# The opening of a hybrid Hyena, grouped-query and neighbourhood attention block: the order of its first loads, its filter taps, and the first halves of two projection tiles

## What is computed

```python
mod_l = (silu(c) @ w_mod + b_mod)          # 6 x 1024 values; c_ctx gives mod_c in the same way
sh1, sc1, gt1, sh2, sc2, gt2 = split(mod_l, 6)
pl = modulate(rms_norm(x, g_mix), sh1, sc1) @ w_in      # h @ w_in, 768 + 512 + 2*128 + 3*256 columns
pc = modulate(rms_norm(ctx, g_mix), csh1, csc1) @ w_in
hy_l, q_l, k_l, v_l, nq_l, nk_l, nv_l = split_proj(pl)
...
# the implicit filter of the Hyena part: a small network over the positions
h = sin(om * (z @ w1 + b1)); h = sin(om * (h @ w2 + b2)); h = sin(om * (h @ w3 + b3))
h = h @ w_out_f                                          # 1024 x 512: 256 forward, 256 backward taps
h_fwd, h_bwd = h[:, :256] * decay, h[:, 256:] * decay
filt = concatenate([h_fwd, zeros(1), h_bwd[:0:-1]])
u = short_conv(hy_l, conv_w, conv_b); v, x1, x2 = split(u, 3); v = v * x1
hyo = x2 * (fft_long_conv(v, filt) + v * skip)
# then: attention of two kinds, output projection, residual, SwiGLU, residual, final rms_norm
```

## Time and profile before

| | us |
|---|---|
| median of 3 runs | 1409.38 |
| lowest and highest | 1409.36, 1409.6 |
| the profiled execution | 1410.57 |
| its span in the trace | 1408.8 |

### The profile page before, as it was taken

One profiled execution on the slowest core, in us unless ns is written; L12 is line 12 of the kernel. 1 busy time (PEld: TensorE's weight loads), 2 busy tenths in 40 slices (PEclk: granted clock), 3 DMA queues, 4 the chain that ended last, 5 costly groups with the idle time before them and its releaser, 6 DMA issues. The chain is left out here.

```text
span 1408.8 us, 24040 instructions
## 1 busy us (share of the span) xinstructions
PE 1341.5 (95%) x8353; PEld 737.0 (52%) x8353; DVE 1003.3 (71%) x1612; ACT 686.8 (49%) x1307; POOL 237.4 (17%) x165
## 2 busy tenths in 40 slices
PE   4989999999888899999899999999999999999997
PEld 0274566444566677777654544444444444444442
DVE  2587677779788889989643697666766665676387
ACT  0442223534577788888630555444444445412235
POOL 0000000133331660000000213333333330000001
PEclk9999999999999999999999999999999999999999
DMA  6916510154140120210011303222222223698953
GB/s 208 375 39 247 201 60 31 61 134 150 31 109 0 32 90 30 63 26 0 2 45 45 90 1 102 78 82 75 81 79 78 82 82 104 229 339 290 339 190 137
DMA packets 119612, 156.25 MB, mean 111 GB/s; under 512 B 18707, under 2 KB 80381, under 8 KB 118269
## 3 DMA queue, kind: packets, MB, share of 16 engines
q1 hardware_dynamic: 113419, 152.32, 32.4%
q10 hardware_dynamic: 6130, 3.11, 0.8%
HBM read 132.98 MB, written 22.42 MB: 110 GB/s over the span
## 5 line engine op out<-in xcount | busy, mean ns | idle before, releaser
L986 PE MATMUL PS<-arena 128*128 128x512 f16 (+6 forms) x7048 | 1218.2, 331 | 35.3 <-DMA arena<-in_hy_f_wout 9.9
L986 PEld LDWEIGHTS PS<-arena 128*128 128x128 f16 (+3 forms) x7048 | 607.5, 102 | 588.4 <-issue 48.2
L2332 DVE SCALAR_TENSOR_TENSOR arena<-arena 128x512 f16<-128x512 f32 x148 | 120.8, 823 | 76.4 <-ACT arena L1747 76.4
L1747 ACT ACTIVATE arena<-arena 128x512 f16<-128x512 f32 x140 | 87.6, 629 | 130.4 <-PE PS L986 130.4
L2268 DVE SCALAR_TENSOR_TENSOR arena<-PS,arena 128x512 f16<-128x512 f32 (+2 forms) x256 | 140.0, 598 | 4.4 <-ACT arena L1686 2.3
L1686 ACT ACTIVATE arena<-PS 128x512 f16<-128x512 f32 (+2 forms) x256 | 118.5, 531 | 49.8 <-PE PS L1271 49.8
L1271 PE MATMUL PS<-arena 128*128 128x128 f32 x864 | 115.2, 278 | 7.4 <-ACT arena L1676 6.0
L1676 ACT ACTIVATE arena<-PS,arena 128x1280 f32<-128x1280 f32 (+1 forms) x96 | 118.0, 1230 | 1.1
L1271 PEld LDWEIGHTS PS<-arena 128*128 128x128 f32 x864 | 93.0, 141 | 44.4 <-ACT arena L1676 43.2
L2260 DVE TENSOR_REDUCE arena<-PS 128x1 f32<-128x1280 f32 x64 | 95.5, 1492 | 23.0 <-PE PS L986 23.0
L1859 ACT ACTIVATE arena<-arena 128x512 f16<-128x512 f32 x77 | 48.1, 629 | 127.3 <-DVE arena L2481 73.4
(11 more groups left out here) (179 smaller groups left out, 1070.7 us busy)
## 6 DMA issues: line engine op xcount, KB each, us to landing
arena<-in_w_ffn_out SPq DMA_DIRECT2D x121, 256.0 KB, 4.8
arena<-in_w_mod SPq DMA_DIRECT2D x24, 1024.0 KB, 6.4
arena<-in_w_ffn_in SPq DMA_DIRECT2D x88, 256.0 KB, 3.0
arena<-in_w_in SPq DMA_DIRECT2D x9, 1024.0 KB, 5.2
left_operands<-arena SPq DMA_DIRECT2D x33, 256.0 KB, 2.2
arena<-left_operands SPq DMA_DIRECT2D x3, 2816.0 KB, 15.1
arena<-in_x SPq DMA_DIRECT2D x2, 2048.0 KB, 17.4
arena<-cst_fwd SPq DMA_DIRECT2D x4, 1024.0 KB, 11.7
```

The lines of the kernel that those rows point to most:

```text
L986: return pe.matmul(out, lhsT, rhs, start=start, stop=stop, skip_group_check=True)
L1747: act.activation(aS[n % RING][:, 0], weight_block(p, b), ACT.Copy, scale=WS).then_inc(blk_hi, 1)
L2332: dve.scalar_tensor_tensor(dst[:, 1], src, WS, dst[:, 0], ALU.mult, ALU.subtract).then_inc(blk_lo, 1)
```

## The change

It has six parts, all in the opening.

1. **Loads.** The vectors c and c_ctx and the identity have a semaphore of their own (`c_in`) and are alone ahead of the chunks. Four `w_mod` chunks follow at once, without the wait for the filter loads; then the other six small loads, and x in front of chunks 5 and 6, `rest` in front of chunk 7. ACT issues three filter loads first, then loads its SiLU table on a dummy value, takes SiLU of c, and only then issues the other seven.
2. **PE's order.** It transposes 16 rows for c alone, takes `modulation(0)` and `(1)`, transposes all 106 rows, takes `modulation(2)`, and only then the first filter layer. The others are spread as shown below.
3. **Taps.** Seven of the eight tap products use the sum and the difference of the filter's output weights (`fwo_sums`, two additions on DVE), so that DVE needs one multiplication per tile in place of three instructions; the first tile keeps the old way.
4. **h.** The first four turns stand ahead of and between the tap products, and DVE splits them between its tap multiplications. `layer_argument`, `normalise_x` and `modulation_gain` move with them.
5. **Hyena.** The first 512 tokens of tiles 0 and 1 (24 products each) are taken after the first six `filter_sums`, with turns 12 to 19 between them; the turns use banks 1 and 3 from n = 12 on (`h_bank`). The second six `filter_sums` follow with nothing between them, then the other halves of both tiles.
6. **Small ones.** DVE takes the first late chunk ahead of the second `filter_spectrum`, the first Hyena weights are split after n = 7 (before: 15), and ACT's two negated copies stand at n = 4.

```diff
-            for dst, src in first:
-                sp.dma_start(dst, src).then_inc(first_in, 16)
+            for dst, src in with_c:
+                sp.dma_start(dst, src).then_inc(c_in, 16)
             n_of = dict.fromkeys(CHUNKS, 0)
             for c in range(N_EARLY):
-                if c == 1:
-
-                    sp.wait_ge(small_in, N_SMALL)
-                if c == 6:
+                if c == 4:
+                    for dst, src in first:
+                        sp.dma_start(dst, src).then_inc(first_in, 16)
+                if c in (5, 6):
+                    i = c - 5
+                    sp.dma_start(xs[:, 4 * i:4 * i + 4], x_rows[:, 4 * i:4 * i + 4]).then_inc(x_in[i], 16)
+                if c == 7:
                     for dst, src in rest:
                         sp.dma_start(dst, src).then_inc(rest_in, 16)
...
-            for dst, src in small:
+            for dst, src in small[:3]:
                 act.dma_start(dst, src).then_inc(small_in, 16)
+            act.wait_ge(pool_own, 1)
+            act.activation(warm, neghalf[:, 0:1], ACT.Silu)
...
+            for dst, src in small[3:]:
+                act.dma_start(dst, src).then_inc(small_in, 16)
...
-            for ct in range(4):
+            pe.wait_ge(hT_f, 20)
+            for ct in range(2):
+                hyena(ct, (1,))
+            for ct in range(2, 4):
                 hyena(ct)
...
+            def tap_tile(nt):
+
+                dve.wait_ge(taps_mm, nt + 1)
+                ps = PS[:, 6 + nt % 2].rearrange("p (a k) -> p a k", a=2)
+                dec = decay[:, nt].rearrange("p (a k) -> p a k", a=2)
+                if nt:
+
+                    dve.tensor_tensor(filt[:, :, nt], ps, dec, ALU.mult).then_inc(taps_rdy, 1)
+                    return
...
             for nt in range(NT):
...
+                tap_tile(nt)
+                if nt == 1:
+                    normalise_x(1, 4, 8)
+                if nt == 3:
+                    mean_x(8, 10)
+                if 2 <= nt < 6:
+                    split_first(nt - 2)
+            normalise_x(2, 8, 10)
```

More of the change, by code:

```diff
@@ L580, in build @@
         ]
+        N_C = len(with_c) * 16
         N_FIRST = len(first) * 16
@@ L1137, in hyena @@
                         for o in others:
-                            for half in range(2):
+                            for half in halves:
                                 ins = mm(PS[:, 2 * b + half, :], w[:, part, k, b * P:b * P + P],
@@ L1141, in hyena, with modulation_columns @@
                                          k == 0 and part + o == 0, k == KD - 1 and part == 1)
-                ins.then_inc(hy_mm, 1)
+                    if between is not None and k % 2 == 1:
+                        turn_h(between + k // 2)
+                if 1 in halves:
+                    ins.then_inc(hy_mm, 1)
+            def modulation_columns(g):
+                pe.wait_ge(mrow_rdy, g + 1)
+                for i in range(8):
+                    o = 16 * g + 2 * i
+                    ins = pe.transpose(PS[:, 5, o:o + 2], mrow[0:2, g, i * P:i * P + P], ident[0:2, 0:2])
+                return ins
@@ new lines, in _ @@
+            pe.wait_ge(silu_rdy, 1)
+            modulation(0)
+            modulation(1)
+            pe.wait_ge(first_in, N_FIRST)
+            pe.transpose(PS[:, 5, 0:N_ROWS], rows[0:N_ROWS], ident[0:N_ROWS, 0:N_ROWS]).then_inc(cols_mm, 1)
+            modulation(2)
+            pe.wait_ge(small_in, N_SMALL)
+            filter_layer(0)
+            modulation(3)
+            modulation(4)
+            pe.wait_ge(cols_rdy, 3)
+            modulation_columns(0)
+            filter_layer(1)
+            modulation(5)
@@ new lines, in _ @@
+            modulation(6)
+            filter_layer(2)
+            modulation(7)
+            turn_h(0)
+            turn_h(1)
+            modulation_columns(1).then_inc(mcol_mm, 1)
+            pe.wait_ge(mlp_h, 3)
+            for nt in range(NT):
+                taps(nt)
+                if nt in (2, 4):
+                    turn_h(1 + nt // 2)
+            n = 4
+            for part, count in enumerate((2, 2, 1, 1, 1, 1)):
+                for i in range(count):
+                    turn_h(n)
+                    n = n + 1
+                if part == 0:
+                    arrived(pe, chunk_index("ff", 0))
+                    pe.wait_ge(mod_rdy, 1)
+                    pe.wait_ge(taps_rdy, NT)
+                if part == 4:
+                    pe.wait_ge(even_part, 2)
+                filter_sums(0, part)
```

228 lines of the change are left out of this document (105 added, 123 removed).

## The result

The changed kernel takes 1422.4 us (1422.1 to 1425.8, 4 runs) against 1409.5 before (1409.4 to 1410.3, 4 runs): a ratio of 1.0096, interval 1.0078 to 1.0113. I had forecast 1401.8, with 1393 to 1413 as the range. The prediction was wrong in sign and outside its range.

A forecast was written before the change was run, and what follows sets the result against it. PE was taken as the engine to follow in the opening. Checkpoint 30 + 81.3 + 6 = 117.3 against 126.9, 9.6 earlier; less 2 for the queue, 7.6: profiled 1410.6 to 1403.0, median 1401.8 us, range 1393 to 1413.

The forecast's parts named there:

- PE before the filter loads: Opening: chunk 0 in at 8.4, three modulation chunks and a transpose follow, so PE reaches the filter layer at 21.9.
- slow start: PE's modulation records after a long idle take 0.86 instead of 0.43 for the first 5.7 us, costing 2.8.
- When the filter loads are in: Landing of the seven filter loads issued at about 5.3: taken as 30, with 21.5 as lower bound and 38.3 as late case.
- S: Time in us when all filter loads are in, taken as 30 (18.48 before); the gain at the checkpoint is 39.6 - S.
- checkpoint: End of the second Hyena tile, where ACT starts on it: 126.9 before, forecast 117.3, before the queue's charge.
- SP's queue goes first: Rival: filter loads move only when SP's queue is dry, S = 50, 10 lost, 1420 us; chance 0.15.
- PE from the landing to the checkpoint: PE's work from S to the end of the second Hyena tile: 81.3 plus 6 of waits in the tap stage.
- The tap sums: Tap stage: DVE needs 0.68 instead of 1.39 per tile for seven of eight, buying room for the splits, not time.
- The spectrum's wait: PE's wait for DVE's spectrum (5.6) goes, covered by 13.8 us of work, and the slow stretch behind it (2.5) too.
- The queue itself: SP's transfers: chunk 7 in at 44.5 to 52.5, wanted by PE at 50.2; 2 us charged.
- Given back: Rival: late chunks on DVE behind the checkpoint return 0.7 to 4 us of the gain, 1402.5 to 1406; chance 0.08.

The follow-up runs named there:

- experiment 2: Changed kernel with the first eight w_mod chunks and both x loads each issued as two transfers of half the columns: 1425.8 us, ratio 1.0113.
- experiment 9: Kernel of experiment 6 plus two unused filling products on PE behind each of the eight tap products: 1392.2 us, ratio 0.9877.
- experiment 12: Changed kernel, doubled loads kept, plus only the unused filling products behind the eight tap products: 1419.7 us, ratio 1.0061.
- version 1: Changed kernel with each of the seven doubled filter loads issued as two transfers of 64 rows: 1399.4 us, ratio 0.9931.
- experiment 7: version 1 with the Hyena halves undone, so tiles are whole again behind the second spectrum's sums: 1408.4 us, ratio 0.9999.
- experiment 6: version 1 with the decay table and four small loads issued after the eighth w_mod chunk instead of ahead of it: 1397.1 us, ratio 0.9919.
- experiment 8: version 1 with the tap sums undone, so DVE multiplies, adds and subtracts for every tile: 1406.9 us, ratio 0.9975.
- experiment 10: Kernel of experiment 6 with the columns' six small loads issued after two w_mod chunks instead of four: 1397.3 us, ratio 0.9892.
- experiment 11: Kernel of experiment 6 with both the filling products and the columns' small loads after two chunks: 1394.1 us, ratio 0.9871.

## Why the prediction was wrong, step by step

*PE before the filter loads.* Forecast 21.9, measured 20.6. Chunk 0 was used at 8.54 (8.4 forecast). The slow start was shorter than forecast: the weight loads of the first records stand 0.86 apart up to 11.5 and 0.43 from there on, so two chunks took 8.32, which is 1.4 over the 6.9 of full pace, where I had 2.8. The six small loads were in at 16.6 (16.8 forecast) and PE's transposition began at 16.79; by my own terms it should have been 18.1 (8.4 + 6.9 + 2.8) and not the 17.6 that I wrote. Nothing rested on it. Right.

*When the filter loads are in.* This is the step that failed, as the prediction put it: "If each of the three further chunks delays them by its own 2.8, S = 29.9 ... I take S = 30". It charged the loads with the chunks' time once. The runs show that they pay per packet: 448 packets on each of two engines, each behind one packet of SP's (12 a us against 127 when spread; 12 against 12 beside the decay table). So they do not finish three chunks later but when SP's queue has run dry, at 43 to 48. By my own formula, 39.6 - S, S = 48.5 gives a loss of 8.9, which is two thirds of the 13.3 at the checkpoint; the other 4.4 arise between the landing and the checkpoint (below). The hint stood in the earlier trace rows: with one chunk in flight ACT got nothing out in the crowded stretch from 8.0 to 10.5. I read this as a delay by the chunk's own time and gave the case of S = 50 only 0.15. The queue's counts of the kernel before told more. From 8 to 10 ACT moved 6 packets beside 204 of SP's, and from 9.67 to 10.31 they came in pairs 0.16 us apart, as in the changed kernel; behind the chunk's last packet they came at over 100 a us.

*The rival "SP's queue goes first"* named the number (S = 50, 1420) but not the mechanism. Under precedence spreading the loads would have won nothing; it won 23 us. The Trainium skill's page "DMA: Bandwidth & Descriptors" (Queues, rings and completion order) says that an engine changes between queues after a whole packet, typically some 9 to 17 descriptors. The order of service is as it says (61 packets against 65 in 10 us), the length of a turn is not: a pair of ACT's every 0.16 us, with one row of SP's between, is a turn of one. From this rule of turns I had concluded that S stays near 30. That did not follow, since I had not counted the packets: at a turn each, 448 of them outlast everything that SP's queue holds.

*PE from the landing to the checkpoint.* Forecast 87.3 (81.3 and 6), measured 91.7, and 91.7 in the kernel of experiment 2 again (144.75 - 53.04). The slow start cost 3.6 (0.31 of 11.5) for 2.8. Idle time from 60 to 90 was 1.2, not 6. In its place stands the half clock of the tap stage: 0.35 x 15 + 0.09 x 17 = 6.8 (from the stretches 75 to 90 and 90 to 107). These make 3.6 - 2.8 + 6.8 - 4.8 = 2.8 of the 4.4; 1.6 I can't place. That the stretch came out only 4.4 off is luck: the idle time that did not come hides most of the slow clock that I had left out. I had reckoned the whole stage at full clock, though the earlier trace rows shows 0.85 there before. Experiments 9 and 12 show that this clock costs time and can be had back.

*The tap sums.* I wrote that they buy room, not time. On version 1 they are worth 4.8 us at the checkpoint, 6.2 by ratio and 7.5 by time: wrong, since a slow DVE also prolongs the slow stretch.

*The spectrum's wait.* Forecast at 5.6 and 2.5 for the slow stretch behind it, 8.1 in all; experiment 7 prices it at 7.7 at the checkpoint and 9 by time. Right in size; the wait reaches PE through ACT and the transposes.

*The queue itself.* Chunk 7 at 44.5 to 52.5, and 2 us of charge: in version 1 it lands at 46.8 and PE waits 3.2. Right, but hidden in the changed kernel by the larger wait.

*Behind the checkpoint.* "Given back": not so, 1279.9 against 1281.9.

## What to carry to other kernels

Before small loads are put beside a full queue, count their packets on the busiest engine and charge each with one packet of the other queue; a load that is confined to two engines by a doubled outer dimension belongs in two transfers. When a chain is tuned to PE's full clock, check the granted clock of the thin stages and not only the waits: here sixteen idle products in the tap stage were worth 3.5 us. A change with good parts (7.7 to 9 us for the Hyena halves, 4.8 to 7.5 for the tap sums, both taken on version 1) can lose through the one that moves transfers, so look at what a removed wait lets through.

## What the hardware showed that I had not expected

- An issue on ACT can stand 13.22 us for a transfer of 256 KB, while its queue holds small packets that take turns with a full one.
- Beside 16 KB packets, 2048-byte packets move at 3 a us on two engines; alone, at 25 a us (112 in 4.5 us).
- A clock that fell to 0.50 (1.2 GHz) in the tap stage stayed there for 14 to 20 us with PE standing at most 1.2 us of it (the changed kernel, experiments 1, 6 and 8), and came back in the full-height products behind the stage.
- The same loads in the same order landed at 48.5 in the changed kernel and at 51.2 in experiment 12; spread, with the columns' loads early, at 20.4 in experiment 10 and at 24.5 in experiment 11.
- Two queues on one DMA engine took turns packet by packet, whatever the packets' sizes: 4 bytes beside 4096 (0.16 us a turn), 2048 bytes beside 16 KB (12 against 12 in 4 us).
